# A quarter of the expert down-projection's columns from gathered rows, four tokens side by side in the array

## The reference

```
expert = jnp.take_along_axis(cand_i, pos, axis=-1)          # [tokens, 8, 16]
g = jax.nn.softmax(top_s, axis=-1)
u = u_emb[expert]
a = jax.nn.gelu(jnp.einsum('thkd,td->thk', u, xb).astype(jnp.float32), approximate=False)
coef = (g * a).astype(xb.dtype)
return jnp.einsum('thk,thkd->td', coef, v_emb[expert])
```

## Time and profile before

| | |
|---|---|
| median of 3 runs | 4169.73 us (4169.28 to 4171.13) |
| span of the profiled execution | 4171.1 us |
| stage v1, first to last matmul start | 1456.99 to 2154.41 us |
| stage v2, first to last matmul start | 3450.37 to 4146.57 us |
| TensorE busy | 4116.5 us, 99% |
| VectorE, ScalarE, GpSimd busy | 3099.3, 2278.5, 516.1 us |
| moved by the DMA engines | 831.31 MB, mean 199 GB/s |

### The profile page before, as it was taken

One profiled execution on the slowest core, in us unless ns is written; L12 is line 12 of the kernel. 1 busy time (PEld: TensorE's weight loads), 2 busy tenths in 40 slices (PEclk: granted clock), 3 DMA queues, 4 the chain that ended last, 5 costly groups with the idle time before them and its releaser, 6 DMA issues.

```text
span 4171.1 us, 72720 instructions
## 1 busy us (share of the span) xinstructions
PE 4116.5 (99%) x21876; PEld 3527.9 (85%) x21876; DVE 3099.3 (74%) x5278; ACT 2278.5 (55%) x4043; POOL 516.1 (12%) x509
## 2 busy tenths in 40 slices
PE   8999999999999999999999999999999999999998
PEld 8978898888888888888889899988888888888887
DVE  6476677885999766777769978688599985566666
ACT  5446544555666655555554465455566665555554
POOL 4100010000222211111100002000022221111110
PEclk9999999999999999999999999999999999999999
DMA  6434656666666666777765545576666666667664
GB/s 223 163 121 150 202 175 194 207 207 197 191 192 191 201 220 219 231 261 246 239 212 178 176 153 184 163 210 206 199 193 190 190 198 221 216 218 238 216 219 161
DMA packets 310247, 831.31 MB, mean 199 GB/s; under 512 B 29040, under 2 KB 129136, under 8 KB 306800
## 3 DMA queue, kind: packets, MB, share of 16 engines
q1 hardware_dynamic: 305184, 812.76, 61.4%
q10 hardware_dynamic: 4944, 17.06, 1.2%
HBM read 779.37 MB, written 50.33 MB: 199 GB/s over the span
## 4 chain that ended last, share of the span: by engine, by line
PE 94%; DVE 4%; ACT 1%; issue 1%; DMA 0%; DVEq 0%; SPq 0%; ACTq 0%
PE psum L419 11%; PE psum L417 11%; PE psum L418 11%; PE psum L485 11%; PE psum L487 11%; PE psum L486 11%; PE psum L1717 5%; PE psum L1719 5%; PE psum L1718 5%; PE psum L1909 2%; PE psum L1911 2%; PE psum L1910 2%; PE psum L408 1%; DVE sb_w_lo L2297 1%; PE psum L426 1%; PE psum L1815 1%
## 5 line engine op out<-in xcount | busy, mean ns | idle before, releaser
L2297 DVE TENSOR_TENSOR sb_w_lo<-sb_raw,sb_w_hi 128x512 fp32r<-128x512 f32 x2736 | 1887.1, 712 | 986.5 <-ACT sb_w_hi L1998 975.5
L1998 ACT CAST sb_w_hi<-sb_raw 128x512 fp32r<-128x512 f32 x2736 | 1696.9, 623 | 1581.2 <-PE psum L487 645.0
L417 PE MATMUL psum<-sb_w_hi,sb_act_hl 128*128 128x512 f32 x2048 | 811.4, 396 | 1.1 <-DVE sb_w_lo L2297 1.1
L419 PE MATMUL psum<-sb_w_lo,sb_act_hl 128*128 128x512 f32 x2048 | 801.5, 391 | 0.0
L418 PE MATMUL psum<-sb_w_hi,sb_act_hl 128*128 128x512 f32 x2048 | 798.9, 390 | 0.0
L485 PE MATMUL psum<-sb_w_hi,sb_act_hl 128*128 128x512 f32 x2048 | 797.0, 389 | 0.8 <-DVE sb_w_lo L2297 0.8
L486 PE MATMUL psum<-sb_w_lo,sb_act_hl 128*128 128x512 f32 x2048 | 796.7, 389 | 0.0
L487 PE MATMUL psum<-sb_w_hi,sb_act_hl 128*128 128x512 f32 x2048 | 796.7, 389 | 0.0
L1717 PE MATMUL psum<-sb_act_hl,sb_w_hi 128*128 128x256 f32 x1488 | 429.8, 289 | 26.9 <-DVE sb_w_lo L2297 13.8
L419 PEld LDWEIGHTS psum<-sb_w_lo,sb_act_hl 128*128 128x128 f32 x2048 | 385.0, 188 | 82.1
L485 PEld LDWEIGHTS psum<-sb_w_hi,sb_act_hl 128*128 128x128 f32 x2048 | 384.4, 188 | 81.0 <-DVE sb_w_lo L2297 1.2
(11 more groups left out here) (377 smaller groups left out, 4240.2 us busy)
## 6 DMA issues: line engine op xcount, KB each, us to landing
sb_raw<-in_u SPq DMA_DIRECT2D x512, 512.0 KB, 4.2
sb_raw<-in_v SPq DMA_DIRECT2D x512, 512.0 KB, 3.5
sb_raw<-in_w_z SPq DMA_DIRECT2D x82, 512.0 KB, 4.3
sb_raw<-in_w_gates SPq DMA_DIRECT2D x64, 512.0 KB, 3.6
sb_acts_in<-acts_mid SPq DMA_DIRECT2D x256, 128.0 KB, 3.3
acts_mid<-sb_acts_out SPq DMA_DIRECT2D x126, 256.0 KB, 5.4
sb_raw<-in_w_proj SPq DMA_DIRECT2D x56, 512.0 KB, 4.2
sb_raw<-in_w_q SPq DMA_DIRECT2D x48, 512.0 KB, 3.8
```

Of the source, the lines that this page charges most:

```text
L417: pe.matmul(ps, h, w_hi[:, c, :], start=k == 0, stop=False)
L419: return pe.matmul(ps, h, w_lo[:, c, :], start=False, stop=k == 15)
L1998: act.copy(w_hi[:, c, :], raw[:, 2 * par + c // 2, (c % 2) * 512:(c % 2) * 512 + 512]).then_inc(hi_ready, 1)
L2297: dve.tensor_tensor(w_lo[:, c, :], raw[:, 2 * par + c // 2, (c % 2) * 512:(c % 2) * 512 + 512], w_hi[:, c, :].bitcast(F32), ALU.subtract). ...
```

## The change

In stage v the dense loop keeps the first 1536 columns (`DENSE`), three quarters per tile; a tile's loads are 512 KB and 256 KB, and the counters still go up by four per tile. The last 512 columns (`PICKED`, PSUM banks 6 and 7) are computed for each token from the rows of its own 128 experts. Those rows (2 KB each) are gathered with indirect DMAs that GpSimd issues, 128 rows for one token, into slots over the unused part of `act_hl` and of `scratch`. For each token the 128 activations are gathered too, one element for each partition, from `acts_mid`. Four tokens whose numbers differ by 32 make a quad, 64 quads per block, with slots for four quads. VectorE multiplies the gathered activations with the softmax weights and places each token's 128 coefficients in one column of a 128 x 32 field of zeros (`place`); TensorE multiplies that with the token's 128 x 512 rows in plain fp32, one token in each group of 32 output columns (`quad`). Quad q comes after tile `quad_tile(q)` = min(5 + 2q, 64 + q, 127). The weighting of the dense field moves from GpSimd to VectorE, which also makes the row numbers for the gathers (`make_indices`). The loops over the tiles of stage v are written out on TensorE and VectorE, and some semaphores are shared to make room for the new ones. The host gives `v_emb` in two arrays.

```diff
+        picked = nc.alloc_sbuf_tensor_at("sb_picked", [P, 14, 512], F32, offset=act_at + 2 * 512 * 4).ap()
...
-            def out_tile(i, par, first):
+            def out_tile(i, k, first=False):
                 pe.wait_ge(c_lo, i + (128 * (blk - 1) + 1))
-                for c in range(4):
+                for c in range(3):
+                    n = down_slot(k, c)
...
-                    mm.then_inc(quarter_used, 1)
-
-            out_tile(0, 0, True)
-            tiles(pe, 1, 128, lambda i, u: out_tile(i, (1 + u) % 2, False))
+                    mm.then_inc(quarter_used, 1 if c < 2 else 2)
+
+            def quad(q):
+
+                n, (t, r) = q % QUAD_SLOTS, divmod(q, 32)
+                pe.wait_ge(lone_ready, QUADS * (blk - 1) + q + 1)
+                for j in range(4):
+                    mm = pe.matmul(psum[32 * j:32 * j + 32, 6 + t, :], lone[:, n, j, :], picked_rows[4 * n + j],
+                                   start=r == 0, stop=False, skip_group_check=True)
+                mm.then_inc(quad_used, 1)
+
+            for i in range(128):
+                out_tile(i, i % 4, i == 0)
+                for q in QUADS_AFTER[i]:
+                    quad(q)
...
+            def make_indices():
+
+                dve.wait_ge(hot_ready, h0 + GROUPS)
...
+            def weigh(i):
+                dve.wait_ge(acts_loaded[i % 2], (i - i % 2) * 8 + (16 + 1024 * (blk - 1)))
+                e = gate_e[:, i, :]
+                dve.tensor_tensor(e, acts_in[:, i % 2, :], e, ALU.mult).then_inc(weighed, 1)
+
+            def place(q):
+
+                n, (t, r) = q % QUAD_SLOTS, divmod(q, 32)
+                dve.wait_ge(picked_loaded[n], 128 * (QUADS // QUAD_SLOTS * (blk - 1) + q // QUAD_SLOTS + 1))
+                if q >= QUAD_SLOTS:
+                    dve.wait_ge(quad_used, QUADS * (blk - 1) + q - QUAD_SLOTS + 1)
+                link(dve.tensor_tensor(picked_coef[:, n, :], by_quad(picked_acts)[:, t, r, :], by_quad(slots[:, 0, :])[:, t, r, :], ALU.mult))
+                wide = [P, 4, 32]
+                dve.tensor_tensor(lone[:, n], picked_coef[:, n, :].unsqueeze(2).broadcast_to(wide),
+                                  one_of[:, 31 - r:63 - r].unsqueeze(1).broadcast_to(wide), ALU.mult).then_inc(lone_ready, 1)
+
+            def lows(i):
+                if i < 127:
+                    weigh(i + 1)
...
+                for q in QUADS_AFTER[i]:
+                    place(q)
...
-                tiles(pool, 0, 128, weigh)
...
+                def pick_rows(q):
+                    n = q % QUAD_SLOTS
+                    for j, at in enumerate(tokens(q)):
+                        pool.indirect_dma_start(picked_rows[4 * n + j], None, v_rows,
+                                                bass.IndirectOffsetOnAxis(ap=v_index[:, at:at + 1], axis=0)).then_inc(picked_loaded[n], 16)
+
+                def pick_acts(q):
+                    n = q % QUAD_SLOTS
+                    for at in tokens(q):
+                        pool.indirect_dma_start(picked_acts[:, at:at + 1], None, acts_flat,
+                                                bass.IndirectOffsetOnAxis(ap=act_index[:, at:at + 1], axis=0)).then_inc(picked_loaded[n], 16)
+
+                pool.wait_ge(index_made, 3 * blk + 1)
+                pool.wait_ge(quarter_used, 4 * base[f"v{blk + 1}"])
+                for q in range(QUAD_SLOTS):
+                    pick_rows(q)
+                for t in range(QT):
+                    pool.wait_ge(acts_stored[t], 16 * UP_GROUPS * (blk + 1))
+                for q in range(QUAD_SLOTS):
+                    pick_acts(q)
+                for q in range(QUAD_SLOTS, QUADS):
+                    pool.wait_ge(quad_used, QUADS * blk + q - QUAD_SLOTS + 1)
+                    pick_rows(q)
+                    pick_acts(q)
...
-    return np.ascontiguousarray(v.reshape(NKEYS, NKEYS, 2, 1024).transpose(1, 2, 0, 3))
+    return np.ascontiguousarray(v[:, 0:DENSE].reshape(NKEYS, NKEYS, DENSE).transpose(1, 0, 2))
```

More of the change, by code:

```diff
@@ L27 @@
 UP_GROUPS = 32
+PICKED = 512
+DENSE = D - PICKED
+QUADS, QUAD_SLOTS = 64, 4
 REPLACED = -3e38
@@ L56, in tile_bases, with quad_tile @@
     return base, evac
+def quad_tile(q):
+    return min(5 + 2 * q, 64 + q, 127)
+QUADS_AFTER = [[q for q in range(QUADS) if quad_tile(q) == i] for i in range(128)]
 def rope_and_masks():
@@ L349, in tiles, with fours, down_slot @@
                 body(first + 2 * turns, 0)
+        def fours(eng, first, last, body):
+            while first % 4 and first < last:
+                body(first, first % 4)
+                first += 1
+            turns = (last - first) // 4
+            if turns > 0:
+                with eng.Fori(0, turns) as turn:
+                    for k in range(4):
+                        body(turn * 4 + (first + k), k)
+            for i in range(first + 4 * max(turns, 0), last):
+                body(i, i % 4)
+        def down_slot(k, c):
+            return (3 * k + c) % 4
         def bank_of(b, first, u):
@@ L603, in high @@
+            def high(i, k):
+                first = isinstance(i, int) and i == 0
+                if not first:
+                    act.wait_ge(quarter_used, i * 4 + (4 * b - 4))
+                act.wait_ge(weighed, i + (128 * (blk - 1) + 1))
+                act.copy(act_hl[:, k % 2, 0:T], gate_e[:, i, :]).then_inc(c_hi, 1)
+                split_down(i, k)
+                if first:
                     gelu(31, 1, last_acts[:, 1, :])
-                    split(b, par, True, (3,))
                     acts_leave(31, 0, acts_out_flat)
@@ L779, in dve_experts @@
+            make_indices()
+            dve.wait_ge(gate_out, GROUPS * blk)
+            weigh(0)
             first = 0
             if blk == 1:
-                tiles(dve, 0, 40, lows)
+                for i in range(0, 40):
+                    lows(i)
                 first = 40
                 for _ in dve_s5_tables(dve, link):
-                    lows(first, first % 2)
+                    lows(first)
                     first += 1
-                tiles(dve, first, 106, lambda i, u: lows(i, (first + u) % 2))
+                for i in range(first, 106):
+                    lows(i)
@@ L787, in dve_experts @@
                 first = 106
                 for _ in dve_s5_inputs(dve, link):
-                    lows(first, first % 2)
+                    lows(first)
                     first += 1
-            tiles(dve, first, 128, lambda i, u: lows(i, (first + u) % 2))
+            for i in range(first, 128):
+                lows(i)
             if blk == 1:
```

142 lines of the change are left out of this document (89 added, 53 removed).

## The result

The changed kernel takes 4351.94 us (median of 4 runs, 4345.85 to 4353.02) where the kernel before takes 4170.43 beside it (4 runs, 4169.28 to 4171.81): a ratio of 1.0431, 95% interval 1.0416 to 1.0446. The forecast was 4000 us, a faster kernel; this one is slower by 4.3%. The time lies inside the range of 3965 to 4510, near the 4325 that rival C had at 1.5 us per gather, but a gather does not take 1.5 us. The profiled execution spans 4351.0 us.

The account below looks back on a forecast made before the run. TensorE, busy 99% of the span, was taken as the bound: 4171.1 - 194.6 + 4 (seams) + 2 (first quads) + 11 (first gathers) + 8 (tables) = 4001.5; runs' median 1.4 lower, so 4000 us. Range: 3965 to 4510.

Parts of the forecast that it names:

- rival C: GpSimd sets the pace: slower above 1.35 us per gather, 4325 us at 1.5; port waits make 1.1 us 1.3; chance 0.44.
- What goes and what TensorE gets: TensorE in the down-projections: 174.1 us per block removed, 64 quads of 1.2 us added, net -97.3 per block.
- D: Quads don't run side by side on TensorE: 3.8 us each, kernel 4312 us; chance 0.06.
- A: TensorE sets the pace, as summed: 3965 to 4030 us, 4000; chance 0.37.
- VectorE: In the down-projections: 6.75 us of work per pair of tiles within 9.36; still fits, with little to spare.
- the sign that I had named for C: In the profile after, VectorE's longest wait would be for the gathered rows, and TensorE's for w_lo.
- The DMA engines: In the down-projections: 308 GB/s, 84 to 94% busy before the single-element packets; it just fits.
- B: DMA engines set the pace: 10 us per pair of tiles, a stage 640 us, kernel 4072 us; chance 0.13.
- The crowding: At the stage's start the first 16 gathers beside dense loads exceed DMA capacity: 5.5 us per block, +11.
- The tables: In block 1's table stretch, 8.4 MB more DMA traffic over 310 us: +8 us.
- The seam: Before the down-projection's first weighting, VectorE makes the indices: 2 us per block, +4.
- GpSimd: 512 indirect DMAs per block at 1.1 us: 563 us, 567 with the landing, under the 600 that TensorE needs.

Follow-up runs that it names:

- no_gathers: Changed kernel without any gather after the first four quads of each block (480 of 512 left out), all quads run on stale data: 4040.35 us.
- no_act_gathers: Changed kernel without the gathers of the tokens' activations (256 of 512 indirect DMAs per block), rows still gathered, all quads run: 4009.45 us.
- tiny_rows: Changed kernel with each row gather after the first four quads bringing 4 bytes a partition instead of 2048, same number of indirect DMAs: 4350.14 us.
- acts_to_memsets: Changed kernel with the activations' gathers replaced by sixteen chained GpSimd writes of zeros per quad: 4176.95 us.
- no_act_pairs: Against no_act_gathers: the row gathers of two quads issued in one run of eight after every second quad: 4015.25 us.
- half_spread: Changed kernel with only tokens 0 to 127 from fetched rows (32 quads, 256 gathers a block), first quads' gathers spread: 4214.36 us, 1.010 of the kernel before.
- half_fours: Against half_spread: GpSimd waits two tiles between a quad's four row gathers and its four activation gathers: 4131.38 us, 0.9908 of the kernel before.
- seven_gathers: Changed kernel with one of each quad's four activation gathers left out, seven indirect DMAs a quad: 4206.7 us.
- half_act_gathers: Changed kernel with two of each quad's four activation gathers left out, six indirect DMAs a quad: 4032.3 us.

## Why the prediction was wrong, point by point

- *What goes and what TensorE gets.* Right. In no_gathers, whose quads all run, the step from quad to quad is 9.39 us (forecast 9.36), and a quad lasts 1.06 us as two rounds of four side by side. D is out. In no_act_gathers a stage is 615 us against 600, and its time of 4009 lies in A's range. So the rest of the sum holds where GpSimd has half the gathers.
- *VectorE.* Right: 290 of 600 us busy, a subtraction 691 ns, and it never waits for gathered rows (in the whole trace 1.1 us in front of a placing, once). So the sign that I had named for C did not show, though GpSimd was behind: its gathers ended some 30 us ahead of their quads, and what stood still were the slots that it waited for.
- *The DMA engines.* Right in size: 310 GB/s at a share of 0.92 in no_act_gathers, without the single-element packets, against 308 and 0.84 to 0.94. B is out; tiny_rows has the same time at 157 GB/s. The crowding was put down to the wrong thing: the start costs some 31 us a block (no_gathers' stages of 632 us against 600; the changed kernel's first quad comes 57 us after the stage's start in block 2, six tiles being 25), not 5.5, and with increments late and the DMA engines 0.58 busy.
- *The tables.* +8 us in block 1: not there; the two stages of no_act_gathers differ by 1 us. *The seam*: +1 us instead of +2.
- *GpSimd.* This is the first step that failed. The term was 1.1 us per gather and 563 us a block, hidden under TensorE's 600. The busy time was near (1.03 to 1.06), but the sum needs the step from one gather to the next, and 0.30 us lie between two of them: 1.34 us. By rival C's own formula, 512 x 1.34 + 4.5 = 691 us, a stage is as long as before, and the kernel some 4160 us. I had read the durations of the nearest rows and not the gaps between them. acts_to_memsets confirms the price of the pace: 703 and 698 us at 10.7 and 10.6 us a quad. This step takes the gain away; it does not make the kernel slower.
- *The waits on TensorE's increments.* This is the second, and it turned the sign. The sum and all four rivals let an increment of TensorE reach the engine that waits for it at once, without saying so; no term or rival had it late. It comes late while GpSimd's indirect DMAs run on. From 705 us (57 to the first quad, 60 rounds of 8 x 1.34, and 5) to the measured 787 is some 80 us a block. That C's 4325 at 1.5 us per gather comes within 27 us of the time is luck: 1.5 is the mean by chance, 12.0 us a quad over eight, while GpSimd's own step is 1.34, and it too stands in front of the late increments, 40 pauses of 2.6 us in block 2. So the loss feeds on itself: late increments hold up the very engine whose gathers make them late, and what it issues next comes in one run again.
- *The clock.* TensorE's busy time is 106 us more than that of no_act_gathers for the same 21364 instructions (4039.2 against 3933.3): by this estimate the lower level after the gaps takes 53 us a block, part of the 80; the granted clock of 0.91 to 0.92 goes with it.

*The 1.3 us per gather of rival C* came near the 1.34, though its parts were other ones. In block 2 of the changed kernel 264 gathers start while VectorE does nothing, and each takes 0.94 to 0.97 us. The 246 that start inside an instruction of VectorE take 1.14 in the mean; where over 0.5 us of that instruction were left, 1.33 (73 of them), where less than 0.2 were left, 0.96. A gather that starts 0.2 us before the end of the second of two subtractions, from the timeline of above:

```profile
3753.11 1.29 DVE L871 TENSOR_TENSOR sb_w_lo<-sb_raw,sb_w_hi 128x512 fp32r<-128x512 f32 x2 [0.31 <-ACT sb_w_hi L654]
...
3754.20 1.03 POOL L2386 DMA_INDIRECT sb_picked<-in_picked_v,sb_slots  x1 [0.30 <-issue]
```

The Trainium skill, "SBUF — State Buffer", section "SBUF: two separate sides", says that a VectorE operation with two SBUF inputs locks a pair of ports against a GpSimd operation that reads SBUF. The trace agrees in kind. In size the wait is 0.09 us per gather in the mean where the prediction had 0.2, and the 1.34 are 0.95, 0.09 and the fixed 0.30.

**What stays open.** Why the increments are late. Shown is that long runs of GpSimd's indirect DMAs bring it (seven or eight in a row of rows and activations, none to speak of with six or four), and that neither the bytes, nor half the indices, nor the quads make a difference. Not shown is that the length of the run is all: the eights of no_act_pairs (rows only, 20 and 30 late, 6 us in all) do much less than the eights of half_spread (rows and activations, 77 and 107 late, some 50 us a block over half_fours). The second has four gathers of single elements behind the rows (seven_gathers has three, half_act_gathers two); it also has four increments of TensorE a tile instead of three and no slot to spare. These were not told apart. All times here come from executions that were recorded, and few updates of TensorE are recorded during a run of gathers even where nothing is late (8 of 117 in the third microsecond of the runs of half_act_gathers); ScalarE's and VectorE's are missing too. So it can't be excluded that the recording takes part in it. The Trainium skill, "NOTIFIC — the notification-queue block", section "Overflow: three behaviours, one of which stalls the engine", says that a full queue of such records can be set up to stall the engine that writes them; no run here shows whether that is so.

## What to carry to other kernels

Price an engine that only issues by its step, gap included, and not by the duration in the profile: here 1.25 us per indirect DMA of GpSimd while VectorE is idle and 1.34 in the mean of these stages, whatever it fetches, and compare the total with the stage at once. Keep indirect DMAs in runs of four, each run tied to a tile of the consumer rather than to the release of a buffer, so that a late start is never caught up in one run. Where a wait is far longer than its cause, compare the end of the instruction that increments with the start of the one that waits. "remote" and "issue" as releasers of several microseconds are a reason to do so and no proof: VectorE's 3.72 us behind "issue" above ended on time.

## What the runs showed of the hardware

- GpSimd: an indirect DMA is 0.94 to 0.97 us busy while VectorE does nothing, 1.14 in the mean when it starts inside an instruction of VectorE, and 1.04 over all, with a gap of 0.30; the same for 128 indices of 2048 bytes and for 128 of 4 bytes, and nearly for 64 indices (0.98 over all); a plain DMA of 256 KB takes 0.57 us.
- Late increments of TensorE, and none seen of ScalarE or VectorE, while seven or eight indirect DMAs follow one another every 9 to 12 us, or eight once in 21 us: up to 12 us from the matmul's end to the waiting engine. With six every 9.4 us next to none.
- Four fp32 products of 32 columns side by side in the array's column groups: eight instructions of 512 columns in 1.06 us, where the prediction's estimate for one by one was 8 x 0.42 us.
